# The opening of an encoder block: norm weights spread by TensorE, weight splits on ScalarE, and another order of loads and turns

## The chip, the cores and the metric

One core of a Trainium2 chip runs the kernel. The metric is the device time in microseconds (us) of one execution; lower is better. The engines run beside each other, each in the order of its own instruction list: TensorE (PE in the profile, its weight loads PEld), VectorE (DVE), ScalarE (ACT), GpSimd (POOL) and SyncE (SP), which issues the DMAs. They meet only at semaphores.

## The reference

One layer of an encoder on x of 1024 tokens by 1024 channels, all in float32:

```python
h = rmsnorm(x, norm_mix)                        # per token, times a gain per channel
proj = h @ w_in
qa, ka, va, ga, cq, ckv, kr, gb = split(proj, [512,128,128,512,384,256,32,512])
ya = window_attention(qa, ka, va, attn_sink) * silu(ga)
q  = rmsnorm(cq, q_a_norm) @ w_uq               # latent path of the second group of heads
kv = rmsnorm(ckv, kv_a_norm) @ w_ukv
yb = latent_attention(q, kv, rope(kr)) * silu(gb)
x  = x + concat(ya, yb) @ w_out
out = rmsnorm(x, final_norm)
```

The change touches only the first line and that part of the second which makes va, cq, ckv and kr.

## The kernel before

Every float32 product is made of three matmuls (`three`, L1097 to L1101): each operand is split into a rounded hi part and a lo part, and hi·hi, hi·lo and lo·hi are added up in PSUM. ps is PSUM, eight banks of 512 columns.

The opening stage works on tiles of 128 tokens, t = 0 to 7, and blocks of 128 input channels, k = 0 to 7.

- SP loads tile t of x into x_in (two buffers, L282) and block k of 800 of w_in's columns (va, ckv, kr, cq) into wn_raw (three buffers, three DMAs per block, L288 to L290). The gain norm_mix is read with each of the 128 partitions getting the whole vector, into g_mix (L293).
- ACT squares a tile with a running sum (L597), DVE makes the variance (L825), ACT the root (L600), DVE the reciprocal (L828) and then the normalised tile x_n, in one instruction over 1024 channels with g_mix (L831, semaphore s_xn).
- PE turns the tile with eight 128x128 transposes into banks 0 and 1 (`turn_x`, L1111; it waits for s_xn and for those banks to be read). ACT copies each half out as hT_hi (`h_hi`, L584), DVE subtracts for hT_lo (`h_lo`, L815, semaphore s_hT).
- POOL splits the weight blocks: wn_hi (L406), then wn_lo (L408, semaphore s_wnr).
- PE multiplies: `natural(t, c, ks)` adds block k of tile t into bank `nat_banks(t)[c]`, with 416 columns for c = 0 (va, ckv, kr) and 384 for c = 1 (cq). Tile t uses banks 2 and 3, 4 and 5, or 6 and 7, by t % 3. Three tiles are worked together, k by k, and between them the later tiles are turned; after k = 5 of the first three tiles all eight tiles have been turned, and k = 6 and 7 of tiles 0, 1 and 2 follow. Then tiles 3 to 7 follow one at a time.
- Tile 3 uses the banks of tile 0. It waits until tile 0's latent parts have been normalised out of them: ACT (L616 to L629), DVE (L851 to L866, semaphore s_lat).

```python
for t in range(3, NT):
    pe.wait_ge(s_hT, 2 * (t + 1))
    pe.wait_ge(s_lat, t - 2)
    natural(t, 0, range(KT))
```

On ACT, the list of the opening ends with `h_hi(NT - 1)` (L603), and the list that reads tile 0's banks begins after it (L613). On DVE it is the same with `h_lo(NT - 1)` (L836) and L848.

After this stage come the up-projections of the latents, windowed attention with the gated projections, latent attention and the output projection.

Of the kernel before, what the change touches and what calls it, by code (L numbers as in the profile page):

```python
# [32 lines left out]
P = 128  # L33
# [26 lines left out]
NA = P + KVL + ROPE  # L60
NW = NA + QL

# [9 lines left out]
def encoder(nc, x, norm_mix, w_in, attn_sink, q_a_norm, w_uq, kv_a_norm, w_ukv, w_out, final_norm,  # L72
# [7 lines left out]
    with ExitStack() as ctx:  # L80
# [21 lines left out]
        g_lat = at("g_lat", 144.5, [P, QL + KVL])  # L102
        lat = at("lat", 147, [P, 2, QL + KVL])
# [62 lines left out]
        ssq, var, rms, rstd = (stat[:, 8 * i:8 * i + 8] for i in range(4))  # L166
        lss, lvar, lrms, lrstd = (stat[:, 32 + 2 * i:34 + 2 * i] for i in range(4))
# [20 lines left out]
        s_wnh, s_wnr = sem("wn_hi_ready"), sem("wn_ready")  # L188
        s_pA, s_pB = sem("natA_done"), sem("natB_done")
# [88 lines left out]
        def _(sp):  # L278
            def load_x(t):
                if t >= 2:  # L280
                    sp.wait_ge(s_xn, t - 1)
                sp.dma_start(x_in[:, t % 2, :], x[t * P:(t + 1) * P, :]).then_inc(s_x[t % 2], 16)  # L282

            def load_wn(k):
                if k >= 3:
                    sp.wait_ge(s_wnr, k - 2)
                rows = w_in[k * P:(k + 1) * P, :]
                sp.dma_start(wn_raw[:, k % 3, 0:P], rows[:, VA:VA + P]).then_inc(s_wn[k % 3], 16)  # L288
                sp.dma_start(wn_raw[:, k % 3, P:NA], rows[:, CKV:CKV + KVL + ROPE]).then_inc(s_wn[k % 3], 16)
                sp.dma_start(wn_raw[:, k % 3, NA:NW], rows[:, CQ:CQ + QL]).then_inc(s_wn[k % 3], 16)  # L290
# [15 lines left out]
            sp.wait_ge(s_wnr, KT)  # L306
# [96 lines left out]
        def _(pool):  # L403
# [176 lines left out]
        def _(act):  # L580
# [10 lines left out]
            for t in range(NT):  # L591
                if t == 3:
                    h_hi(t - 1)
# [3 lines left out]
                nc.scalar.activation(x_n[:, t % 2, :], x_in[:, t % 2, :], ACT.Square,  # L597
                                     accum_out=ssq[:, t:t + 1]).then_inc(s_ssq, 1)
                act.wait_ge(s_var, t + 1)
                nc.scalar.activation(rms[:, t:t + 1], var[:, t:t + 1], ACT.Sqrt).then_inc(s_rms, 1)  # L600
                if t >= 1 and t != 3:
                    h_hi(t - 1)
            h_hi(NT - 1)  # L603
# [9 lines left out]
            for t in range(NT):  # L613
                a, b = nat_banks(t)
                act.wait_ge(s_pA, t + 1)
                nc.scalar.activation(vA[:, t, :, 0:HD], ps[:, a, 0:P].rearrange("p (g c) -> p g c", c=HD),  # L616
                                     ACT.Copy)
                if t >= 2:
                    act.wait_ge(s_lT, t - 1)
                nc.scalar.activation(lat[:, t % 2, QL:QL + KVL], ps[:, a, P:P + KVL], ACT.Square,  # L620
                                     accum_out=lss[:, 1:2])
                nc.scalar.activation(kr_n[:, t, :], ps[:, a, P + KVL:NA], ACT.Copy).then_inc(s_va, 1)
                act.wait_ge(s_pB, t + 1)
                nc.scalar.activation(lat[:, t % 2, 0:QL], ps[:, b, 0:QL], ACT.Square,
                                     accum_out=lss[:, 0:1]).then_inc(s_lss, 1)
# [177 lines left out]
        def _(dve):  # L803
# [17 lines left out]
            for t in range(NT):  # L821
                if t == 3:
                    h_lo(t - 1)
                dve.wait_ge(s_ssq, t + 1)
                nc.vector.tensor_scalar(var[:, t:t + 1], ssq[:, t:t + 1], 1.0 / D, EPS, ALU.mult,  # L825
                                        ALU.add).then_inc(s_var, 1)
                dve.wait_ge(s_rms, t + 1)
                link(nc.vector.reciprocal(rstd[:, t:t + 1], rms[:, t:t + 1]))  # L828
                if t == 0:
                    dve.wait_ge(s_gmix, 16)  # L830
                nc.vector.scalar_tensor_tensor(out=x_n[:, t % 2, :], in0=x_in[:, t % 2, :],  # L831
                                               scalar=rstd[:, t:t + 1], in1=g_mix[:, :], op0=ALU.mult,
                                               op1=ALU.mult).then_inc(s_xn, 1)
                if t >= 1 and t != 3:
                    h_lo(t - 1)
# [12 lines left out]
            for t in range(NT):  # L848
# [12 lines left out]
                nc.vector.scalar_tensor_tensor(out=lat[:, t % 2, 0:QL], in0=ps[:, b, 0:QL],  # L861
                                               scalar=lrstd[:, 0:1], in1=g_lat[:, 0:QL], op0=ALU.mult,
                                               op1=ALU.mult)
                nc.vector.scalar_tensor_tensor(out=lat[:, t % 2, QL:QL + KVL], in0=ps[:, a, P:P + KVL],
# [231 lines left out]
        def _(pe):  # L1096
# [7 lines left out]
            def turn_x(t):  # L1104
                pe.wait_ge(s_xn, t + 1)
                for a in range(2):
                    if t >= 1:
                        pe.wait_ge(s_hT, 2 * t - 1 + a)
                    for k in range(4):
                        c = 4 * a + k  # L1110
                        last = nc.tensor.transpose(ps[:, a, k * P:(k + 1) * P], x_n[:, t % 2, c * P:(c + 1) * P],  # L1111
                                                   ident[:, :])
                    last.then_inc(s_xT, 1)


            def natural(t, c, ks):
# [3 lines left out]
                for k in ks:  # L1120
                    last = three(ps[:, nat_banks(t)[c], 0:w1 - w0], hT_hi[:, k, toks], hT_lo[:, k, toks],
# [14 lines left out]

            pe.wait_ge(s_id, 2)

            turn_x(0)
            turn_x(1)  # L1140
# [12 lines left out]
            for t in range(3):  # L1153
                for c in range(2):
                    natural(t, c, range(KT - 2, KT))
# [256 lines left out]
```

## Time and profile before

| | |
|---|---|
| time before, median of 3 runs | 655.77 us (654.43 to 657.53) |
| profiled execution, first to last instruction | 655.6 us; no other time is given for it |
| PE busy | 633.3 us, 97% of the span |
| DVE busy | 403.8 us, 62% |
| ACT busy | 330.8 us, 50% |
| POOL busy | 302.5 us, 46% |
| idle before the turns of x on PE (L1111) | 7.9 us and 3.7 us |

The busy time of PE says how long matmuls were in flight, not how fast they went: its clock has two levels, and a matmul counts as busy at either. A line of the timeline gives the start in us, the length, the engine, the source line, the operation and its tiles; square brackets hold the idle time just before it and what ended that.

### The profile page before, as it was taken

The page shows a single profiled execution, that of the slowest core. Times are in us where ns is not written, and L with a number is a line of the kernel's source. Part 1 is how long each engine was busy: PE and PEld are TensorE (multiplying, and loading weights), DVE is VectorE, ACT ScalarE, POOL GpSimd, SP SyncE. Part 2 cuts the span into 40 slices and gives each one's busy share as a digit, 9 for nine tenths or more (in the row PEclk, how much of TensorE's full clock was granted, in tenths as well). Part 3 has the DMA queues.
Part 4 walks back from the last instruction along what each step waited for, and adds up shares of the span by engine and source line. Part 5 has one row for each costly group of instructions (what it writes and reads, how often), then busy time and mean ns, then how long its engine had stood idle before and what let it go on. Part 6 is the DMA issues. An engine that isn't in the chain of part 4 may idle for free.

```text
span 655.6 us, 8923 instructions
## 1 busy us (share of the span) xinstructions
PE 633.3 (97%) x3252; PEld 538.6 (82%) x3252; DVE 403.8 (62%) x773; ACT 330.8 (50%) x717; POOL 302.5 (46%) x283
## 2 busy tenths in 40 slices
PE   3999999999999999999999999999999999999996
PEld 2999998888888888788877788888888887888884
DVE  4753317333221158888885988888888888855422
ACT  4542222223222147777774877777777778404312
POOL 4962004402323244363535676886787777820000
PEclk9899999999999999999999999999999999999999
DMA  7730006363121210100123101011013201403521
GB/s 239 236 116 0 1 13 244 140 255 107 34 64 33 64 33 1 32 2 1 48 71 100 32 10 41 4 38 41 1 41 98 104 1 33 160 1 122 178 86 64
DMA packets 31612, 47.38 MB, mean 72 GB/s; under 512 B 2544, under 2 KB 19440, under 8 KB 31440
## 3 DMA queue, kind: packets, MB, share of 16 engines
q1 hardware_dynamic: 31568, 46.81, 22.7%
q8 instruction: 26, 0.43, 0.3%
q14 instruction: 18, 0.15, 0.1%
HBM read 35.13 MB, written 11.67 MB: 71 GB/s over the span
## 4 chain that ended last, share of the span: by engine, by line
PE 88%; DVE 6%; ACT 2%; DMA 1%; issue 1%; SPq 0%; DVEq 0%; ACTq 0%
PE ps L1099 21%; PE ps L1101 21%; PE ps L1100 21%; PE ps L1308 8%; PE ps L1324 4%; PE ps L1325 4%; PE ps L1251 2%; DVE p_w L934 2%; PE ps L1241 2%; PE ps L1252 1%; DVE pT_wl L962 1%; DVE o_w L972 1%; PE ps L1111 1%; DMA g_mix<-norm_mix 1%; DVE Y L921 1%
## 5 line engine op out<-in xcount | busy, mean ns | idle before, releaser
L523 POOL TENSOR_SCALAR p_b<-p_b,stat 128x1024 f32<-128x1024 f32 x64 | 72.0, 1126 | 52.8 <-DVE stat L1023 52.3
L738 ACT ACTIVATE pT_hi<-ps 128x512 fp32r<-128x512 f32 x128 | 69.9, 596 | 38.5 <-PE ps L1308 38.4
L1018 DVE TENSOR_REDUCE stat<-ps 128x1 f32<-128x1024 f32 x64 | 77.6, 1213 | 10.1 <-PE ps L1101 10.1
L1099 PE MATMUL ps<-hT_hi,w_hi 128*128 128x512 f32 x208 | 83.6, 402 | 0.0
L1028 DVE TENSOR_TENSOR pT_lo<-ps,pT_hi 128x512 fp32r<-128x512 f32 x128 | 81.8, 680 | 1.4 <-ACT pT_hi L738 1.4
L1101 PE MATMUL ps<-hT_hi,w_lo 128*128 128x512 f32 x208 | 81.3, 391 | 0.0
L1100 PE MATMUL ps<-hT_lo,w_hi 128*128 128x512 f32 x208 | 81.1, 390 | 0.0
L729 ACT ACTIVATE p_b<-ps,stat 128x1024 f32<-128x1024 f32 x64 | 71.5, 1117 | 12.0 <-DVE stat L1018 11.7
L1308 PEld LDWEIGHTS ps<-ident,p_b 128*128 128x128 f32 x512 | 59.3, 141 | 12.1 <-issue 2.6
L1308 PE MATMUL ps<-ident,p_b 128*128 128x128 f32 x512 | 67.3, 273 | 1.0 <-DVE pT_lo L1028 0.9
L466 POOL TENSOR_SCALAR p_w<-p_w,stat 128x384 f32<-128x384 f32 (+1 forms) x48 | 28.1, 602 | 60.9 <-DVE stat L949 60.9
L406 POOL TENSOR_SCALAR w_hi<-w_raw 128x1024 fp32r<-128x1024 f32 x13 | 14.1, 1083 | 91.1 <-PE ps L1101 91.1
L1324 PE MATMUL ps<-pT_hi,vB 128*128 128x512 f32 x128 | 55.3, 432 | 0.0
L1101 PE MATMUL ps<-k_hi,q_lo 96*128 96x512 f32 x128 | 50.5, 394 | 0.0
L1100 PE MATMUL ps<-k_lo,q_hi 96*128 96x512 f32 x128 | 50.5, 394 | 0.0
L1099 PE MATMUL ps<-k_hi,q_hi 96*128 96x512 f32 x128 | 50.3, 393 | 0.0
L1325 PE MATMUL ps<-pT_lo,vB 128*128 128x512 f32 x128 | 50.3, 393 | 0.0
L1101 PE MATMUL ps<-wo_hi,y_lo 128*128 128x512 f32 x128 | 49.8, 389 | 0.0
L1100 PE MATMUL ps<-wo_lo,y_hi 128*128 128x512 f32 x128 | 49.8, 389 | 0.0
L1099 PE MATMUL ps<-wo_hi,y_hi 128*128 128x512 f32 x128 | 49.8, 389 | 0.0
L1099 PE MATMUL ps<-wn_hi,hT_hi 128*128 128x384 f32 (+1 forms) x128 | 46.3, 362 | 0.0
L1101 PEld LDWEIGHTS ps<-hT_hi,w_lo 128*128 128x128 f32 x208 | 39.0, 188 | 8.5
(155 smaller groups left out, 1430.5 us busy)
## 6 DMA issues: line engine op xcount, KB each, us to landing
w_raw<-w_in SPq DMA_DIRECT2D x13, 512.0 KB, 3.9
x_in<-x SPq DMA_DIRECT2D x8, 512.0 KB, 4.5
wo_raw<-w_out SPq DMA_DIRECT2D x8, 512.0 KB, 4.0
x_r<-x SPq DMA_DIRECT2D x8, 512.0 KB, 3.9
out<-o_n SPq DMA_DIRECT2D x16, 256.0 KB, 2.3
q_nope_scratch<-stage SPq DMA_DIRECT2D x8, 256.0 KB, 2.9
k_nope_scratch<-stage SPq DMA_DIRECT2D x8, 256.0 KB, 2.1
v_scratch<-stage SPq DMA_DIRECT2D x8, 256.0 KB, 2.0
```

Of the source, the lines that this page charges most:

```text
L466: nc.gpsimd.tensor_scalar(p_w[:, u % 2, r, 0:w], p_w[:, u % 2, r, 0:w], w_col(5, u)[:, r:r + 1], 0.5, ALU.mult, ALU.mult).then_inc(s_wp, 1)
L523: nc.gpsimd.tensor_scalar(p_b[:, (U + 1) % 4, :], p_b[:, (U + 1) % 4, :], r_b[:, U % 4:U % 4 + 1], 0.5, ALU.mult, ALU.mult).then_inc(s_bp, 1)
L729: nc.scalar.activation(p_b[:, (U + 1) % 4, :], ps[:, b:b + 2, :].rearrange("p b c -> p (b c)"), ACT.Exp, bias=nm_b[:, U % 4:U % 4 + 1], ac ...
L738: nc.scalar.activation(pT_hi[:, G % 2, 4 * a:4 * a + 4, U % 4 * P:(U % 4 + 1) * P], ps[:, 4 + a, :].rearrange("p (k c) -> p k c", c=P), AC ...
L1018: nc.vector.tensor_reduce(nm_b[:, U % 4:U % 4 + 1], ps[:, b:b + 2, :].rearrange("p b c -> p (b c)"), AX.X, ALU.max, negate=True).then_inc( ...
L1028: nc.vector.tensor_tensor(pT_lo[at_], ps[:, 4 + a, :].rearrange("p (k c) -> p k c", c=P), f(pT_hi[at_]), ALU.subtract).then_inc(s_bTl, 1)
L1099: nc.tensor.matmul(o, a_hi, b_hi, start=first, stop=False)
L1100: nc.tensor.matmul(o, a_hi, b_lo, start=False, stop=False)
L1101: return nc.tensor.matmul(o, a_lo, b_hi, start=False, stop=last)
L1308: last = nc.tensor.transpose(ps[:, 4 + a, k * P:(k + 1) * P], p_b[:, (U + 1) % 4, (4 * a + k) * P:(4 * a + k + 1) * P], ident[:, :])
L1324: nc.tensor.matmul(o, vB[:, hp, k, :], pT_hi[:, G % 2, k, :], start=(k == 0), stop=False)
L1325: last = nc.tensor.matmul(o, vB[:, hp, k, :], pT_lo[:, G % 2, k, :], start=False, stop=(k == NT - 1))
```

## The change

- norm_mix is loaded as 8 rows of 128 (g_row, 4 KB). PE turns it to a column layout in bank 3, DVE copies it out (g_col), and PE spreads it with eight transposes of a broadcast column over banks 6 and 7. Tile 0 is normalised with the gain read from PSUM; ACT copies the two banks to g_mix for the other tiles (`keep_g`).
- Tile 0's squares are made half on ACT and half on DVE. All tiles are normalised in two instructions of 512 channels, each with its own increment of s_xn, and `turn_x` waits for each half.
- wn_hi is made by ACT (`wn_hi_k`), wn_lo by POOL in two parts (512 and 288 columns).
- The columns are divided anew: c = 0 holds va and cq (512), c = 1 holds ckv and kr (288); a block is loaded by two DMAs, not three. The steps that read the banks follow.
- Loads, ACT's list and PE's list stand in a new order. PE also does 8 and 4 transposes (`spin`) whose results nothing reads. The last turns of x are now spread among k = 4 to 7, and `turn_x(7)` is the last thing before tile 3.

```diff
-NA = P + KVL + ROPE
-NW = NA + QL
+NA = P + QL
+NW = NA + KVL + ROPE
...
             load_x(0)
-            sp.dma_start(g_mix[:, :], norm_mix.partition_broadcast(P)).then_inc(s_gmix, 16)
+            sp.dma_start(g_row[:, :], norm_mix.rearrange("(k c) -> k c", c=P)).then_inc(s_grow, 16)
+            load_wn(0)
             load_x(1)
-            load_wn(0)
             load_wn(1)
+            load_wn(2)
             load_x(2)
-            load_wn(2)
-            for t in range(3, NT):
-                load_wn(t)
-                load_x(t)
+            load_wn(3)
+            load_x(3)
+            load_wn(4)
+            load_wn(5)
+            load_x(4)
+            load_wn(6)
+            load_x(5)
+            load_wn(7)
+            load_x(6)
+            load_x(7)
...
             for k in range(KT):
-                pool.wait_ge(s_wn[k % 3], 48 * (k // 3 + 1))
-                split(wn_raw[:, k % 3, :], wn_hi[:, k, :], wn_lo[:, k, :], s_wnh, k + 1, s_wnr)
+                pool.wait_ge(s_wnh, k + 1)
+                for w0, w1 in ((0, NA), (NA, NW)):
+                    nc.gpsimd.tensor_tensor(wn_lo[:, k, w0:w1], wn_raw[:, k % 3, w0:w1], f(wn_hi[:, k, w0:w1]),
+                                            ALU.subtract).then_inc(s_wnr, 1)
...
+            def wn_hi_k(k):
+                act.wait_ge(s_wn[k % 3], 32 * (k // 3 + 1))
+                nc.scalar.activation(wn_hi[:, k, :], wn_raw[:, k % 3, :], ACT.Copy).then_inc(s_wnh, 1)
+
+            def keep_g(a):
+                act.wait_ge(s_xn, a + 1)
+                nc.scalar.activation(g_mix[:, a * HALF:(a + 1) * HALF], ps[:, 6 + a, :],
+                                     ACT.Copy).then_inc(s_gmix, 1)
+
+            square_x(0)
+            wn_hi_k(0)
+            keep_g(0)
+            h_hi(0)
+            keep_g(1)
+            square_x(1)
+            wn_hi_k(1)
+            h_hi(1)
+            wn_hi_k(2)
+            square_x(2)
...
+            square_x(7)
+            h_hi(6)
+            h_hi(7)
...
+            dve.wait_ge(s_gT, 1)
+            nc.vector.tensor_copy(g_col[:, :], ps[:, 3, 0:KT]).then_inc(s_gcol, 1)
+            for t in range(4):
+                norm_x(t)
+                if t < 3:
+                    h_lo(t)
+            for t in range(4, NT):
+                norm_x(t)
+                h_lo(t - 1)
...
             pe.wait_ge(s_id, 2)
+            spin(8)
+            pe.wait_ge(s_grow, 16)
+            nc.tensor.transpose(ps[:, 3, 0:KT], g_row[:, :], ident[0:KT, 0:KT]).then_inc(s_gT, 1)
+            pe.wait_ge(s_gcol, 1)
+            for a in range(2):
+                for k in range(4):
+                    last = nc.tensor.transpose(ps[:, 6 + a, k * P:(k + 1) * P],
+                                               g_col[:, 4 * a + k:4 * a + k + 1].to_broadcast([P, P]), ident[:, :])
+                last.then_inc(s_gb, 1)
+            spin(4)
 
             turn_x(0)
+            both(0, (0,))
             turn_x(1)
-            for k in range(KT - 2):
-                for t in range(3):
-                    if k == 0:
-                        pe.wait_ge(s_hT, 2 * (t + 1))
-                    pe.wait_ge(s_wnr, k + 1)
-                    for c in range(2):
-                        natural(t, c, range(k, k + 1))
-                    if k == 0 and t == 0:
-                        turn_x(2)
-                if k >= 1:
-                    turn_x(2 + k)
-            pe.wait_ge(s_wnr, KT)
-            for t in range(3):
-                for c in range(2):
-                    natural(t, c, range(KT - 2, KT))
+            both(0, (1,))
+            both(1, (0, 1))
+            both(0, (2,))
+            both(1, (2,))
+            turn_x(2)
+            both(0, (3,))
+            both(1, (3,))
+            both(2, range(4))
+            turn_x(3)
+            for k in range(4, KT):
+                for t in range(3):
+                    both(t, (k,))
+                turn_x(k)
             for t in range(3, NT):
                 pe.wait_ge(s_hT, 2 * (t + 1))
                 pe.wait_ge(s_lat, t - 2)
```

`both(t, ks)` is `natural(t, 0, ...)` and `natural(t, 1, ...)` for each k of ks.

## Rows read from the trace of the kernel before

**Rows 1.** The page: busy time of each engine over the span.
```profile
PE 633.3 (97%) x3252; PEld 538.6 (82%) x3252; DVE 403.8 (62%) x773; ACT 330.8 (50%) x717; POOL 302.5 (46%) x283
```

**Rows 2.** Waits of PE, whole span: us in total, times, longest.
```profile
PE ps L1111 <- DVE x_n L831: 7.9, 1, 7.9
PE ps L1111 <- DVE hT_lo L815: 3.7, 2, 2.0
PE ps L1251 <- DVE pT_wl L962: 1.4, 4, 0.5
```

**Rows 3.** The chain of waits, 0 to 20 us: start, length, what.
```profile
1.18 5.19 DMA g_mix<-norm_mix
...
6.48 1.29 DVE x_n L831
...
7.79 4.35 DMA x_in<-x
...
13.97 2.50 DVE x_n L831
16.47 0.61 DVE hT_lo L815
...
17.22 1.24 PE ps L1111 x8
```

**Rows 4.** Timeline, 4 to 26 us.
```profile
4.03 1.06 ACT L597 ACTIVATE x_n<-x_in 128x1024 f32<-128x1024 f32 x1 [1.80 <-DMA x_in<-x]
5.00 0.19 ACT L597 ACTIVATION_READ_ACCUMULATOR x_n<-x_in 128x1 f32 x1
5.21 0.15 DVE L825 TENSOR_SCALAR stat<-stat 128x1 f32<-128x1 f32 x1 [5.21 <-ACT x_n L597]
5.40 0.20 ACT L600 ACTIVATE stat<-stat 128x1 f32<-128x1 f32 x1 [0.22 <-DVE stat L825]
5.64 0.17 DVE L828 RECIPROCAL stat<-stat 128x1 f32<-128x1 f32 x1 [0.27 <-ACT stat L600]
...
7.91 1.94 PE L1111 MATMUL ps<-ident,x_n 128*128 128x128 f32 x8 [7.91 <-DVE x_n L831]
...
8.83 0.86 POOL L406 TENSOR_SCALAR wn_hi<-wn_raw 128x800 fp32r<-128x800 f32 x1 [7.36 <-DMA wn_raw<-w_in]
...
9.56 1.28 DVE L831 SCALAR_TENSOR_TENSOR x_n<-x_in,stat,g_mix 128x1024 f32<-128x1024 f32 x1
...
14.91 0.34 PE L1101 MATMUL ps<-wn_hi,hT_lo 128*128 128x384 f32 x1
```

**Rows 5.** Groups by shape, 0 to 50 us: busy in all, mean ns of one, idle before.
```profile
L408 POOL TENSOR_TENSOR wn_lo<-wn_raw,wn_hi 128x800 fp32r<-128x800 f32 x8 | 17.0, 2128 | 0.7
...
L815 DVE TENSOR_TENSOR hT_lo<-ps,hT_hi 128x512 fp32r<-128x512 f32 x16 | 10.3, 686 | 6.7 <-ACT hT_hi L584 6.6
...
L584 ACT ACTIVATE hT_hi<-ps 128x512 fp32r<-128x512 f32 x16 | 8.8, 595 | 13.7 <-PE ps L1111 13.6
```

**Rows 6.** Busy time and granted clock (the number before the last two) by stretch.
```profile
18.20:21.50 3.30, 3.30 (x12) 3.20 (x11) 2.34 (x5) 2.12 (x5) 3.22 (x3) 0.50 0.88 285
22.00:26.00 4.00, 4.00 (x26) 3.93 (x25) 2.57 (x4) 1.25 (x4) 3.92 (x2) 1.00 0.52 158
```

**Rows 7.** Timeline, 37 to 50 us.
```profile
37.73 1.04 PE L1111 MATMUL ps<-ident,x_n 128*128 128x128 f32 x8
38.37 1.09 ACT L584 ACTIVATE hT_hi<-ps 128x512 fp32r<-128x512 f32 x2 [1.61 <-PE ps L1111]
38.53 0.43 PE L1099 MATMUL ps<-wn_hi,hT_hi 128*128 128x416 f32 x1
...
44.10 0.28 ACT L616 ACTIVATE vA<-ps 128x128 fp32r<-128x128 f32 x1 [0.48 <-PE ps L1101]
...
45.15 0.49 ACT L624 ACTIVATE lat<-ps 128x384 f32<-128x384 f32 x1 [0.32 <-PE ps L1101]
...
46.98 0.47 DVE L864 SCALAR_TENSOR_TENSOR lat<-ps,stat,g_lat 128x256 f32<-128x256 f32 x1
...
47.13 0.35 PE L1099 MATMUL ps<-wn_hi,hT_hi 128*128 128x416 f32 x1
...
49.32 0.35 PE L1099 MATMUL ps<-wn_hi,hT_hi 128*128 128x416 f32 x1
```

More of the change, by code:

```diff
@@ L102, in encoder @@
         g_lat = at("g_lat", 144.5, [P, QL + KVL])
+        g_row = at("g_row", 201, [KT, P])
+        g_col = at("g_col", 204, [P, KT])
         lat = at("lat", 147, [P, 2, QL + KVL])
@@ L590, in _, with square_x @@
             nc.scalar.activation(oss[:, 0:1], ident[:, 0:1], ACT.Sqrt)
-            for t in range(NT):
-                if t == 3:
-                    h_hi(t - 1)
+            def square_x(t):
                 act.wait_ge(s_x[t % 2], 16 * (t // 2 + 1))
@@ L596, in _ @@
                     act.wait_ge(s_xT, 2 * (t - 1))
-                nc.scalar.activation(x_n[:, t % 2, :], x_in[:, t % 2, :], ACT.Square,
-                                     accum_out=ssq[:, t:t + 1]).then_inc(s_ssq, 1)
+                if t == 0:
+                    nc.scalar.activation(x_n[:, 0, 0:HALF], x_in[:, 0, 0:HALF], ACT.Square, scale=D ** -0.5,
+                                         accum_out=ssq[:, 0:1]).then_inc(s_ssq, 1)
+                else:
+                    nc.scalar.activation(x_n[:, t % 2, :], x_in[:, t % 2, :], ACT.Square,
+                                         accum_out=ssq[:, t:t + 1]).then_inc(s_ssq, 1)
                 act.wait_ge(s_var, t + 1)
                 nc.scalar.activation(rms[:, t:t + 1], var[:, t:t + 1], ACT.Sqrt).then_inc(s_rms, 1)
-                if t >= 1 and t != 3:
-                    h_hi(t - 1)
-            h_hi(NT - 1)
+            def wn_hi_k(k):
[15 more added lines that the diff above has]
+            square_x(2)
+            wn_hi_k(3)
+            h_hi(2)
+            wn_hi_k(4)
+            square_x(3)
+            wn_hi_k(5)
+            square_x(4)
+            h_hi(3)
+            wn_hi_k(6)
+            square_x(5)
+            h_hi(4)
+            wn_hi_k(7)
+            square_x(6)
+            h_hi(5)
+            square_x(7)
+            h_hi(6)
+            h_hi(7)
             def lat_hi(t):
@@ L818, in h_lo, with norm_x @@
                                             ALU.subtract).then_inc(s_hT, 1)
[L821 to L826, printed above, removed]
+            def norm_x(t):
+                if t == 0:
+                    dve.wait_ge(s_x[0], 16)
+                    link(nc.vector.tensor_tensor_reduce(out=x_n[:, 0, HALF:], in0=x_in[:, 0, HALF:],
+                                                        in1=x_in[:, 0, HALF:], scale=1.0 / D, scalar=EPS,
+                                                        op0=ALU.mult, op1=ALU.add, accum_out=sq_b))
+                    dve.wait_ge(s_ssq, 1)
+                    nc.vector.tensor_tensor(var[:, 0:1], ssq[:, 0:1], sq_b, ALU.add).then_inc(s_var, 1)
+                else:
+                    dve.wait_ge(s_ssq, t + 1)
+                    nc.vector.tensor_scalar(var[:, t:t + 1], ssq[:, t:t + 1], 1.0 / D, EPS, ALU.mult,
+                                            ALU.add).then_inc(s_var, 1)
@@ L827, in _ @@
                 dve.wait_ge(s_rms, t + 1)
                 link(nc.vector.reciprocal(rstd[:, t:t + 1], rms[:, t:t + 1]))
[L829 to L835, printed above, removed]
+                for a in range(2):
+                    cols = slice(a * HALF, (a + 1) * HALF)
+                    if t == 0:
+                        dve.wait_ge(s_gb, a + 1)
+                        gain = ps[:, 6 + a, :]
+                    else:
+                        dve.wait_ge(s_gmix, a + 1)
+                        gain = g_mix[:, cols]
+                    nc.vector.scalar_tensor_tensor(out=x_n[:, t % 2, cols], in0=x_in[:, t % 2, cols],
+                                                   scalar=rstd[:, t:t + 1], in1=gain, op0=ALU.mult,
+                                                   op1=ALU.mult).then_inc(s_xn, 1)
```

45 lines of the change are left out of this document (29 added, 16 removed).

## The prediction

> **What bounds the kernel now.** I read the page first: PE is busy for 97% of the span, everything else for 62% or less [rows 1]. So only time in which PE stands still or runs slowly can be won. The waits of PE say where it stands still: 7.9 us before the first turn of x and 3.7 us before the next two; the next entry, far later, is 1.4 us in all [rows 2]. The change can win only in the first 17 us. The chain of waits names what is late there, in turn: the 512 KB of g_mix, DVE's first x_n, tile 2 of x, and DVE's x_n of tile 2, which took 2.50 us where the neighbouring one in the timeline took 1.28 [rows 3, 4]. From 17.22 on PE has work without a break.
>
> The third view is the clock. In the stretch 18.2 to 21.5 the granted clock is 0.50, the lower level, and in 22 to 26 it is 1.00 [rows 6]; before it fell PE had stood still from 15.25 to 17.22 [rows 3, 4]. At the lower level 12 matmuls started in 3.3 us, at the upper 26 in 4.0, or 21.5 in 3.3. The 9.5 missing ones at 0.154 us are 1.5 us, and over a whole low stretch of some 3.5 us about 1.7. The first eight transposes took 1.94 us, those at 37.73 1.04 [rows 4, 7]: the opening also runs slowly.
>
> A yardstick: `natural` of tile 3 begins at 49.32 [rows 7]. From 17.22 to there PE did six turns and 23 of the 24 (tile, k) pairs of the first three tiles, in 32.1 us, of which 1.7 us is the low clock: 30.4 us of work at full clock. What the change does to this 49.32 it does to the end, since PE is without notable waits after it.
>
> **The change part by part.**
>
> *Size of the matmuls.* Twelve of them (two pairs) take 49.32 - 47.13 = 2.19 us [rows 7], 1.09 us a pair. 512 + 288 columns are as many as 416 + 384. One of 400 columns on average takes 0.1825, of which 0.167 are its columns at 2.4 GHz, the upper level, and 0.016 are fixed; 288 columns would need 0.12 + 0.016. I take no change; if a matmul of 288 columns cost as much as one of 384, it would be 3 x 0.04 us (96 columns) x 64 pairs = 7.7 us. Against that speaks that a weight load and its 128-column transpose go through in 1.04/8 = 0.13 us [rows 7], no more than 288 columns need anyway, so a load does not hold them up. I give 0, upper end +1 us.
>
> *The first tile.* g_mix landed at 6.37; without it x_n(0) would have been possible at 5.8 [rows 3, 4]. In its place: x_in lands at 4.03, g_row behind it, at 4.1 to 4.2; a turn (0.4), DVE's copy (0.2), and four transposes at the slow rate (1.2) make the first half of the gain ready at 6.1, the second at 6.9. DVE first has to wait for the turned g_row, and only then sums its half of the squares (0.7, as a 512-wide operation of L815), so the variance comes at 5.7, the root at 6.1, the reciprocal at 6.3. The halves of x_n(0) end at 7.0 and 7.7. The spins end at 7.5, and the turn begins there: 0.4 us earlier than 7.91. The change does what its first item says, but the 512 KB were replaced by a chain nearly as long. Bounds: 7.1 (spin at full clock) to 9.0 (g_row as late as g_mix's 6.37 [rows 3]; I take 4.2, since it is 4 KB and not 512).
>
> *ACT's list, what is late next.* Behind tile 0's root (6.1) come now wn_hi(0) (0.85: 800 columns between 0.56 for 512 and 1.06 for 1024 [rows 4, 5]; to 6.95), keep_g(0) (from 7.0, to 7.6), h_hi(0) (its halves wait for the turn, 8.65 and 9.5 at the slow rate; to 10.1), keep_g(1) (to 10.6), and only then the square of tile 1, which has lain in x_in since about 6.6. Square to x_n ready to start took 4.03 to 5.83, 1.8 us [rows 4]: x_n(1) runs from 12.4 to 13.8. Before, it ran from 9.56 to 10.84 [rows 4]. Tile 1 is thus 3 us later than before; tile 2, which held PE up before, no longer does (x_n(2) at 18.2 to 19.5 against a turn at 20). wn_hi(1) follows at 12.2, wn_lo(1) on POOL ends in two parts at 14.3 and 15.1 (2.1 us in all [rows 5]). Turn 1 is done at 14.1 to 14.6, and the pair (0, k=1) can start at about 14.6. Bounds: 13.9 with everything before at full clock, 16.0 if DVE's halves and POOL stretch each other as the 2.50 us instruction shows [rows 3].
>
> *From there.* Six turns and 23 pairs are left, the same as at 17.22 before. I followed the lists on: wn_lo(2) at 17.6 and 18.4 against 17.9 and 18.6; hT(2) at 21.9 against 23.1; the turns of tiles 3 to 7 and the blocks k = 4 to 7 are ready 1.5 to 4 us ahead. Moving wn_hi to ACT takes 8 x 1.35 us from POOL, which then waits on ACT; ACT has room (8.8 us of copies in 50). The x loads now stand behind weight loads in SP's queue, which wait for s_wnr; x(4) goes out at about 20 for a square at 27. No cover is lost. So the work ends at 14.6 + 30.4 = 45.0 without any low clock, 46.7 with the same 1.7 us as before; I take 45.9. That is 3.4 us ahead of 49.32.
>
> *The stall before tile 3.* Before, the last turn was at 41.89 and twelve pairs' worth of matmuls, 6.6 us, stood behind it before tile 3. Now `turn_x(7)` is the last thing before it. ACT's and DVE's lists read tile 0's banks only behind h_hi(7) and h_lo(7), which wait for that very turn; and tile 3 waits for tile 0's latents. So a chain that had lain under matmuls lies open. With S the start of the turn: h_hi(7) ends at S + 1.73 (37.73 to 39.46); PE would go on at S + 0.80 (38.53) [rows 7]. From vA's start to the end of the last latent instruction took 44.10 to 47.45, 3.35 us, with 0.32 us of waiting for PE in it [rows 7], so 3.03. PE goes on at S + 1.73 + 3.03 + 0.1 = S + 4.85 and has stood still 4.05 us. The new division of columns orders the same instructions otherwise, to the same sum. The only cover is none; the bounds are 3.7 and 4.4.
>
> *The clock behind the stall.* A stop of 1.97 us was followed by a low stretch worth 1.7 us [rows 3, 4, 6]. This stop is twice as long, so I charge 1.7 again; lower bound 0.
>
> *Sum.* Tile 3 effectively begins at 45.9 + 4.05 + 1.7 = 51.65 against 49.32: +2.3 us. The span is 655.6 and the median of the runs 655.77, so nothing is lost between the two; 655.77 + 2.3 = 658.0.
>
> One point on the clock could move this. In the trace the lower rate held through 16 transposes and ended at about 14.5, a bit over a microsecond after the first matmuls of the pairs had begun; that the transposes helped to raise the clock is likely, since they made up most of what PE had done, but one trace does not prove it. The Trainium skill, "TensorE: Matmul & The Clock Gate", Part 4, says that transposes do not count as PE activity for the clock in the way matmuls do. By that rule the spins and the spreading of the gain raise nothing, and the opening is slow throughout; what that costs here is the third rival.
>
> **The rivals.**
> 1. *Forecast: stall and low clock outweigh the earlier start.* Around +2.3 us, 656.5 to 659.5. Chance 0.45.
> 2. *Full clock all through; not slower.* PE is nearly without a break from 4.9 to 9.3 us in the new list. If that brings the upper level before 9 us, and the stop before tile 3 does not cost it, the work starts at 13.9, ends at 44.3, and tile 3 begins at 48.4: -1.0 us, 654.8. It decides at a low-clock cost under 1 us in all. For it: after 14.5 the full rate came and lasted over a 2 us stop, until 18.2. Against: it then fell. Chance 0.2. A gain of over 0.5% needs the stall to be absent as well, by a cover that I overlook: 3.4 to 5 us ahead, 651.5; chance 0.05.
> 3. *Transposes leave the clock low; slower.* Turns 0 and 1 and the first pairs at half rate: start at 15.3, the full 1.7 us, end at 47.4; then 4.05 and 1.7: 53.15, +3.8 us, 659.6. The page named above is the reason to hold this apart. For it: the first 16 transposes were all slow, and the clock fell at 18.2 after turns and a stop. Chance 0.2.
> 4. *POOL and DVE in each other's way.* x_n halves and wn_lo stretched as in the 2.50 us case: start at 16.0, +1.4 us on the forecast, 659.5 or, with rival 3, 661. Chance 0.1.
>
> **How the numbers follow.** About 0.5% (3.3 us) is what a measurement of this kernel tells from no change; the three runs before lie 3.1 us apart. Slower by more than that, over 659.1: nearly all of rivals 3 and 4 (0.28) and a tenth of the forecast's case, 0.33. Faster by more, under 652.5: 0.05. The same: the rest, 0.62. The range 653.8 to 661.2 reaches from rival 2, with the spread of the runs below it, to rivals 3 and 4 together.
>
> **What would show it.** Right: PE's waits show one new entry of about 4 us before L1099 at 45 to 47 us, ended by DVE's latents (L930 or so), the granted clock is low after it, and the first wait before a turn ends at 7.5. ACT's square of tile 1 starts at 10 to 11 us, not on landing. Wrong: no such entry; or a second stop between 16 and 45 us, which would mean that ACT's list is the bound; or the first pairs already at the full rate, which would make rival 2 true; or 288-column matmuls spaced wider than 0.14 us.

## The result and the profile after

The changed kernel takes 662.67 us (661.97 to 662.71, 4 runs) against 656.54 us of the kernel before (654.43 to 657.53, 4 runs): a ratio of 1.0092, 95% interval [1.0077, 1.0107]. It is slower by 6.1 us. Forecast were 658.0 us and +2.3 us; the sign and the stall were right, the price of the low clock was not, and the time lies above the range. The profiled executions are 660.9 and 655.6 us long, 5.3 us apart.

The page of the changed kernel, busy time of each engine, beside [rows 1]:

```profile
PE 640.7 (97%) x3273; PEld 536.6 (81%) x3273; DVE 405.6 (61%) x784; ACT 337.0 (51%) x727; POOL 292.6 (44%) x283
```

Waits of PE in the changed kernel (us in total, times, longest), beside [rows 2]:

```profile
PE ps L1166 <- DVE lat L931: 3.9, 1, 3.9
PE ps L1178 <- DVE x_n L890: 2.6, 2, 1.7
```

The 7.9 and 3.7 us before the turns have become 2.6 (and 1.5 before the first spin, which costs nothing). A new entry stands on top: 3.9 us before the first matmul of tile 3 (L1166), ended by DVE's latents. It is the stall that the prediction placed there.

Timeline of the opening, beside [rows 3, 4]:

```profile
5.88 1.52 DVE L890 SCALAR_TENSOR_TENSOR x_n<-x_in,stat,ps 128x512 f32<-128x512 f32 x2
...
7.27 1.91 PE L1178 MATMUL ps<-ident,x_n 128*128 128x128 f32 x8
...
9.74 0.50 PE L1166 MATMUL ps<-wn_hi,hT_hi 128*128 128x512 f32 x1 [0.56 <-DVE hT_lo L862]
...
10.19 1.06 ACT L611 ACTIVATE x_n<-x_in 128x1024 f32<-128x1024 f32 x1
...
11.99 2.42 DVE L890 SCALAR_TENSOR_TENSOR x_n<-x_in,stat,g_mix 128x512 f32<-128x512 f32 x2
...
15.24 0.78 PE L1166 MATMUL ps<-wn_hi,hT_hi 128*128 128x512 f32 x1
...
15.81 0.63 PE L1167 MATMUL ps<-wn_lo,hT_hi 128*128 128x512 f32 x1
...
16.24 0.63 PE L1168 MATMUL ps<-wn_hi,hT_lo 128*128 128x512 f32 x1
...
20.14 0.39 PE L1168 MATMUL ps<-wn_hi,hT_lo 128*128 128x512 f32 x1
```

The reader is to see four things. The turn of tile 0 starts at 7.27, 0.6 us earlier than before. The first pair, at 9.74, already runs at the full rate (0.23 us between its 512-column matmuls). ACT squares tile 1 only at 10.19, and its two normalising instructions, beside POOL's wn_lo, take 2.42 us, where the same two of a later tile took 1.41 (at 35.01, with POOL idle); before, x_n(1) was ready at 10.84, now at 14.4. And the matmuls from 15.24 on are 0.43 us apart instead of 0.23: they run at half rate until 20.14. By the granted clock the low stretch is longer: it begins at 13.2 and ends at 20.0. (In the first microseconds that column is no guide: it reads 1.00 from 5 to 9 us, where the transposes were 0.21 us apart, against 0.11 at full rate in experiment 1. There the rate is read from the spacing.)

Timeline around the stall, beside [rows 7]:

```profile
46.98 1.03 PE L1178 MATMUL ps<-ident,x_n 128*128 128x128 f32 x8
...
48.59 0.28 ACT L663 ACTIVATE vA<-ps 128x128 fp32r<-128x128 f32 x1
...
51.27 0.47 DVE L931 SCALAR_TENSOR_TENSOR lat<-ps,stat,g_lat 128x256 f32<-128x256 f32 x1
...
51.89 0.77 PE L1166 MATMUL ps<-wn_hi,hT_hi 128*128 128x512 f32 x1 [3.88 <-DVE lat L931]
...
57.57 0.40 PE L1167 MATMUL ps<-wn_lo,hT_hi 128*128 128x512 f32 x1
```

Turn of tile 7 at 46.98, tile 0's first copy on ACT behind h_hi(7) at 48.59, the last latent instruction at 51.27, tile 3 at 51.89 and not 49.32. From there 13 matmuls of 512 columns take 5.68 us, to 57.57. Busy time by stretch, the granted clock being the number before the last two, beside [rows 6]:

```profile
15.20:19.80 4.60, 4.60 (x15) 3.94 (x14) 2.14 (x5) 3.36 (x6) 2.57 (x3) 0.50 0.60 203
...
48.00:51.70 3.70, 0.02 (x1) 0.00 (x0) 2.83 (x9) 3.09 (x15) 3.42 (x10) 0.87 0.01 2
51.70:57.20 5.50, 5.31 (x13) 4.18 (x14) 1.54 (x7) 0.37 (x2) 5.50 (x8) 0.50 0.00 0
```

At full rate (0.23 us apart) the 13 would take 3.0 us, so this low stretch costs 2.7 us. The one in the opening, 15.24 to 20.14, holds 8 matmuls of 512 and 6 of 288 columns, 8 x 0.23 + 6 x 0.13 = 2.6 us of work in 4.9: 2.3 us lost.

The account by the yardstick: tile 3 begins 2.57 us later than before, its first matmuls lose 2.7 us more, together 5.3 us, which is the whole difference of the two profiled executions.

### The profile page after: what moved, and what is told of

It is laid out like the page before. It is cut to its first block, busy times and chain, and to the rows that moved or that the text cites. A ratio compares the mean times of both kernels' runs of the same rounds, so it can differ in the third digit from the quotient of the medians.

```text
span 660.9 us, 8993 instructions
## 1 busy us (share of the span) xinstructions
PE 640.7 (97%) x3273; PEld 536.6 (81%) x3273; DVE 405.6 (61%) x784; ACT 337.0 (51%) x727; POOL 292.6 (44%) x283
## 4 chain that ended last, share of the span: by engine, by line
PE 89%; DVE 6%; ACT 2%; issue 2%; DMA 0%; SPq 0%; DVEq 0%; ACTq 0%
PE ps L1166 21%; PE ps L1168 21%; PE ps L1167 21%; PE ps L1400 8%; PE ps L1417 4%; PE ps L1416 4%; PE ps L1343 2%; DVE p_w L1001 2%; PE ps L1333 2%; PE ps L1344 1%; PE ps L1178 1%; DVE pT_wl L1029 1%; DVE o_w L1039 1%; PE ps L1322 1%; PE ps L1321 1%
## 5 line engine op out<-in xcount | busy, mean ns | idle before, releaser
L1085 DVE TENSOR_REDUCE stat<-ps 128x1 f32<-128x1024 f32 x64 | 77.6, 1213 | 10.2 <-PE ps L1168 10.1
L1166 PE MATMUL ps<-hT_hi,w_hi 128*128 128x512 f32 x208 | 83.6, 402 | 0.0
L1166 PE MATMUL ps<-wn_hi,hT_hi 128*128 128x288 f32 (+1 forms) x128 | 47.4, 370 | 4.4 <-DVE lat L931 3.9
L1166 PE MATMUL ps<-k_hi,q_hi 96*128 96x512 f32 x128 | 50.3, 393 | 0.0
L1166 PE MATMUL ps<-wo_hi,y_hi 128*128 128x512 f32 x128 | 49.8, 389 | 0.0
```

The source lines that it names most:

```text
L1085: nc.vector.tensor_reduce(nm_b[:, U % 4:U % 4 + 1], ps[:, b:b + 2, :].rearrange("p b c -> p (b c)"), AX.X, ALU.max, negate=True).then_inc( ...
L1166: nc.tensor.matmul(o, a_hi, b_hi, start=first, stop=False)
```

## The experiments

All times are medians; the ratios are to the kernel before on the same chip, which took 657.3 to 657.4 us in these three groups of runs, with their 95% intervals. Experiments 1, 2 and 4 to 6 make one edit to the changed kernel and 3 makes one to the kernel before; the others build on 2 and 8. The changed kernel was not run again in these groups: in its own group the kernel before took 656.54. So a difference "under the changed kernel" compares two groups and is sure to about 1 us; the spans of the traces and the starts inside them are given beside it where it matters.

**1. Two pairs of cover.** The turns of tiles 4 to 7 one place earlier.

```diff
             for k in range(4, KT):
                 for t in range(3):
                     both(t, (k,))
-                turn_x(k)
+                    if t == 0:
+                        turn_x(k)
```

> The changed kernel, but the turns of tiles 4 to 7 stand behind the first of the three pairs of their k instead of the third, so two pairs (2.2 us) of matmuls cover the chain before tile 3. Theory (the stall and the low clock behind it are the loss): the stop before tile 3 shrinks from 3.9 to about 1.7 us, 2.2 us less; if the clock then stays up, 2.6 us more are won: 2.2 to 4.8 us under the changed kernel. Rival (the opening is what costs, the turns are needed as late as they are): a new stop before the turns of tiles 4 to 7 takes the place of the one removed and the time stays within 1 us of the changed kernel.

657.4 us, ratio 1.0006 [0.9997, 1.0015]: 5.3 us under the changed kernel, and level with the kernel before. Its waits of PE:

```profile
PE ps L1178 <- DVE x_n L890: 2.4, 2, 1.3
PE ps L1166 <- DVE lat L931: 1.7, 1, 1.7
```

The stop before tile 3 is 1.7 us, tile 3 begins at 49.03, and the clock stays at 1.00 from 18.2 us on. 2.2 us fewer of stop and 2.7 us of low clock make 4.9 us; the spans are 5.5 apart (655.4 against 660.9). The other 0.6 are of the opening, where this execution's low stretch is shorter (14.7 to 18.1) though its first 20 us are the same code. The rival falls: the waits before turns did not grow.

**2. Four pairs of cover.**

```diff
-                turn_x(k)
+                    if t == 0 and k < 7:
+                        turn_x(k)
+                    if t == 1 and k == 6:
+                        turn_x(7)
```

> The changed kernel, but the turn of tile 7 already behind the second pair of k = 6, the turns of 4 to 6 behind the first pair of their k: four pairs (4.4 us) cover the chain before tile 3. Theory: no stop before tile 3 and no low clock after it, 3.9 + 2.6 = 6.5 us under the changed kernel, which is then 0 to 1.5 us under the kernel before. Rival: the turns come too early, PE waits before them instead, and no more than half is won.

657.28 us, 1.0004 [0.9994, 1.0013], 5.4 us under the changed kernel. The stop before tile 3 is 0.7 us. The expected 6.5 us were not reached; beyond the first two pairs of cover nothing measurable is added. The rival does not explain it: the waits before the turns are 2.3 us, against 2.6 in the changed kernel. The 0.7 us that are left of the stop are not the turn's any more, as ACT's first copy out of tile 0's bank shows:

```profile
46.59 0.28 ACT L663 ACTIVATE vA<-ps 128x128 fp32r<-128x128 f32 x1 [1.19 <-PE ps L1168]
```

It waits for the last matmul of tile 0, behind which the new order has two pairs before tile 3, where the kernel before had four. And the opening goes two ways: five of the ten runs, with a mean granted clock (over the whole run) of 0.993 or 0.994, took 657.5 to 658.1 us, the other five (0.996 to 0.998) 656.4 to 657.0. The profiled one is of the first kind, low from 12.6 to 19.5 us. So in this form, without the turn's stall, the rest of the change is worth about nothing, not the 3.4 us by which I had put it ahead.

**3. The stall alone, in the kernel before.**

```diff
-                if k >= 1:
+                if 1 <= k < 5:
                     turn_x(2 + k)
             pe.wait_ge(s_wnr, KT)
             for t in range(3):
                 for c in range(2):
                     natural(t, c, range(KT - 2, KT))
+            turn_x(7)
```

> The kernel before with one edit: the turn of tile 7 is moved behind all 24 pairs, directly ahead of tile 3. Theory: 4 us of stop and 1.7 to 2.6 us of low clock, 5.7 to 6.6 us slower than the kernel before, as much as the whole change costs. Rival (the stall is harmless, because PE is ahead of something else later): under 2 us slower.

662.09 us, 1.0084 [1.0062, 1.0106], 4.7 us over the kernel before by the medians, 5.5 by the ratio; a little less than I expected. One moved turn costs nearly as much as the whole change. The new entry among the waits of PE, then the stretches of the stop and behind it:

```profile
PE ps L1099 <- DVE lat L864: 3.6, 1, 3.6
```

```profile
48.80:52.40 3.60, 0.02 (x1) 0.00 (x0) 2.96 (x9) 3.09 (x15) 3.35 (x9) 1.00 0.01 2
53.00:57.00 4.00, 4.00 (x15) 3.84 (x14) 1.08 (x3) 0.04 (x1) 4.00 (x7) 0.59 0.01 4
```

A stop of 3.6 us, then a granted clock of 0.59 on average over 4 us (0.41 x 4 = 1.6 us lost), at a place where the kernel before has neither: the stall brings the low clock with it. The opening of this run is the code of the kernel before, and in this trace it has no low stretch, where that of the kernel before has one from 18.2 to 21.6 us [rows 6].

**4. Filling the stall.** Matmuls that nothing reads, on bank 0 as soon as it is free.

```diff
                 turn_x(k)
+            pe.wait_ge(s_hT, 2 * NT - 1)
+            for _ in range(12):
+                nc.tensor.matmul(ps[:, 0, :], hT_hi[:, 0, 0:P], wn_hi[:, 0, 0:HALF], start=True, stop=True)
```

> The changed kernel with 12 matmuls of 512 columns, whose results nothing reads, in the stop before tile 3 (from when bank 0 is free, about 1 us into it, to its end). Theory (the low clock is a cost of its own, caused by PE standing still): the stretch at a granted clock of 0.50 after the stop goes, the start of tile 3 stays where it is or comes up to 0.3 us later, and the kernel is 2.3 to 2.6 us faster than the changed one. Rival (the low clock there comes by itself, or from something else that happens then): no gain, or a loss by the extra matmuls.

659.73 us, 1.0037 [1.0023, 1.005], 2.9 us under the changed kernel:

```profile
48.74 2.99 PE L1250 MATMUL ps<-wn_hi,hT_hi 128*128 128x512 f32 x12 [0.98 <-DVE hT_lo L862]
51.63 0.47 PE L1166 MATMUL ps<-wn_hi,hT_hi 128*128 128x512 f32 x1
51.94 0.40 PE L1167 MATMUL ps<-wn_lo,hT_hi 128*128 128x512 f32 x1
```

PE does work for nothing from 48.74 on, tile 3 starts 0.3 us earlier than in the changed kernel, and its matmuls are 0.23 us apart from the second on. The low clock behind the stop is a cost of its own, of 2.7 us by the trace and 2.9 by the times, and it is PE's standing still that causes it. (The opening has its low stretch here too, 12.6 to 19.4 us, and in four of the five runs the mean granted clock is 0.992; the fifth, with 0.999, took 658.5 us.)

**5. Filling the gap of the opening.**

```diff
             both(0, (0,))
+            for _ in range(7):
+                nc.tensor.matmul(ps[:, 4, :], hT_hi[:, 0, 0:P], wn_hi[:, 0, 0:HALF], start=True, stop=True)
             turn_x(1)
```

> The changed kernel with 7 matmuls of 512 columns, whose results nothing reads, between the first pair and the turn of tile 1, where PE stands still for 1.7 us. Theory (the low stretch from about 14 to 20 us is caused by PE standing still for the halves of tile 1): the granted clock stays at 1.00, the pairs from 15 us on go at full rate, and up to 2.3 us are won against the changed kernel. Rival (the clock falls there whatever PE does in that gap, or the second gap alone brings it down): within 0.5 us of the changed kernel.

659.16 us, 1.0021 [1.0012, 1.0031], 3.5 us under the changed kernel. Two pieces of PE's timeline:

```profile
10.71 1.78 PE L1235 MATMUL ps<-wn_hi,hT_hi 128*128 128x512 f32 x7
...
14.28 0.48 PE L1166 MATMUL ps<-wn_hi,hT_hi 128*128 128x512 f32 x1
14.60 0.39 PE L1167 MATMUL ps<-wn_lo,hT_hi 128*128 128x512 f32 x1
```

```profile
48.96 0.77 PE L1166 MATMUL ps<-wn_hi,hT_hi 128*128 128x512 f32 x1 [3.88 <-DVE lat L931]
...
52.08 0.42 PE L1167 MATMUL ps<-wn_lo,hT_hi 128*128 128x512 f32 x1
```

The pairs from 14.28 on run at full rate, against half rate until 20.14 in the changed kernel. The stall is as long as ever (48.96 is its end), but the low stretch behind it is shorter: 7 matmuls in 3.12 us, 1.5 us lost instead of 2.7. The profiled execution is 4.1 us shorter than the changed kernel's (656.8 against 660.9): tile 3 begins 2.9 us earlier, and 1.2 less is lost behind the stall. Of the 2.9, about 2 are the clock from the second pair on; that pair also starts 1.0 us earlier, but not because of the edit alone, since in experiment 1, without it, it started at 14.37. What a stop of 3.9 us costs in clock is not one number: 1.5 and 2.7 us were seen. Both forms of the rival are out: with the gap of 1.7 us filled the clock stays up in this trace and in that of experiment 7, though the second gap (1.0 us) is still there, while all four traces with the gap as it was (the changed kernel, experiments 1, 2 and 4) have a low stretch.

**6. Without the spins.**

```diff
             pe.wait_ge(s_id, 2)
-            spin(8)
...
-            spin(4)
```

> The changed kernel without the 8 and the 4 spins. Theory (transposes do raise the clock; in the changed kernel the first pair at 9.7 us went at the full rate with nothing but transposes before it): the first pair goes at the half rate and the turn of tile 0 starts 0.2 us earlier; the time changes by less than 1 us, since PE waits for tile 1 anyway. Rival (spins do nothing at all): the first pair still at the full rate, no change of time.

659.77 us (658.65 to 662.45), 1.0043 [1.0026, 1.006], 2.9 us under the changed kernel, where I expected less than 1 us either way. PE's timeline:

```profile
6.63 1.97 PE L1178 MATMUL ps<-ident,x_n 128*128 128x128 f32 x8
9.15 0.80 PE L1166 MATMUL ps<-wn_hi,hT_hi 128*128 128x512 f32 x1 [0.56 <-DVE hT_lo L862]
9.75 0.63 PE L1167 MATMUL ps<-wn_lo,hT_hi 128*128 128x512 f32 x1
...
16.52 0.30 PE L1168 MATMUL ps<-wn_hi,hT_lo 128*128 128x288 f32 x1
...
50.00 0.47 PE L1166 MATMUL ps<-wn_hi,hT_hi 128*128 128x512 f32 x1 [3.88 <-DVE lat L931]
50.30 0.39 PE L1167 MATMUL ps<-wn_lo,hT_hi 128*128 128x512 f32 x1
...
54.18 0.39 PE L1168 MATMUL ps<-wn_hi,hT_lo 128*128 128x512 f32 x1
```

The first pair is at half rate (0.43 us between the 512-column matmuls, 0.23 with spins), as the theory had it. But the clock comes up at 16.5 and stays, while with spins it came up before 9.7, fell before 14 and was low until 20.14. My reading is that the spins raise the clock too early for a PE that then stands still for 1.7 us (0.7 here, where the slower matmuls and transposes fill the time). Only part of the gain is of the opening, though. By the traces (658.0 against 660.9 us) tile 3 begins 1.9 us earlier, and the rest lies behind the stall: ten steps from 50.30 to 54.18 take 3.9 us instead of 2.3, 1.6 us lost instead of 2.7. And it is partly luck: six of the eight runs took 658.65 to 660.37 us with a mean granted clock of 0.995 or 0.996, but two took 661.9 and 662.45 us with 0.988 and 0.987, the time and the clock of the changed kernel (0.988 in all four of its runs).

**7. Cover and filling together.** The edits of 2 and 5.

> The turns of e2_four_pairs together with the filling matmuls of e5_fill_opening. Theory (two causes that add up): 6.0 us (cover, as measured in e2) and up to 2.3 us (clock in the opening) under the changed kernel, so 1 to 2 us under the kernel before. Rival (the opening's clock is made up for by waits behind it): the same time as e2_four_pairs, within 0.5 us.

655.64 us, 0.9965 [0.9952, 0.9978], 7.0 us under the changed kernel and 1.6 us under e2. Each edit is worth something beside the other, and this is the first version under the kernel before. But they do not simply add up: alone they brought 5.4 and 3.5 us, and what the filling wins behind the stall cannot be won again where the stall is covered. Tile 3 begins at 47.27.

**8. Tile 1's squares on DVE.** With the turns of 2, without filling matmuls.

```diff
             keep_g(0)
             h_hi(0)
-            keep_g(1)
             square_x(1)
+            keep_g(1)
             wn_hi_k(1)
...
                 norm_x(t)
+                if t == 0:
+                    dve.wait_ge(s_x[1], 16)
+                    nc.vector.tensor_tensor_reduce(out=x_n[:, 1, :], in0=x_in[:, 1, :], in1=x_in[:, 1, :],
+                                                   scale=1.0 / D, scalar=EPS, op0=ALU.mult, op1=ALU.add,
+                                                   accum_out=var[:, 1:2]).then_inc(s_var, 1)
```

(`square_x(1)` keeps only the root, and `norm_x(1)` no longer makes the variance.)

> The turns of e2_four_pairs, and tile 1's squares made on DVE instead of ACT, with ACT's root for tile 1 straight behind the hi halves of tile 0. Theory (ACT's list is what holds tile 1 back: its square started at 10.2 though the tile had landed before 8): x_n of tile 1 starts at 10.6 to 11 instead of 12.0, the second pair 1.0 to 1.6 us earlier, PE's gap is shorter and the clock may stay up: 1 to 3.5 us under e2_four_pairs. Rival (wn_lo of block 1 on POOL holds the second pair, not tile 1): x_n(1) earlier, but the second pair no more than 0.5 us earlier and no gain.

654.4 us, 0.9947 [0.9933, 0.9962]: 8.3 us under the changed kernel, 2.9 under e2, 2.9 under the kernel before. Timeline:

```profile
7.79 1.40 DVE L903 CUSTOM_DVE_ANT_0 x_n<-x_in 128x1024 f32<-128x1024 f32 x1 [0.34 <-DMA x_in<-x]
...
10.63 2.43 DVE L893 SCALAR_TENSOR_TENSOR x_n<-x_in,stat,g_mix 128x512 f32<-128x512 f32 x2
...
13.53 0.48 PE L1174 MATMUL ps<-wn_hi,hT_hi 128*128 128x512 f32 x1
...
13.85 0.39 PE L1175 MATMUL ps<-wn_lo,hT_hi 128*128 128x512 f32 x1
```

The squares start when tile 1 lands (7.79), x_n(1) at 10.63 and not 11.99, the second pair at 13.53 (14.37 to 15.29 in the four traces with the old opening) and at full rate. Tile 3 begins at 46.12. The rival falls, and ACT's list was what held the opening back.

**9. Experiment 8 without the spins** (the diff of 6).

> e8_squares_on_dve without its 12 spins. Theory (the spins do raise the clock, and in the changed kernel they only raised it too early to last): the first pair and the turn of tile 1 go at half rate and the clock comes up near 16 us, as in e6_no_spins; 1 to 2 us slower than e8. Rival (spins only cost): as fast as e8 or faster.

654.7 us, 0.9956 [0.9942, 0.9971]; the interval overlaps that of e8, which is from another group (the kernel before took 657.28 and 657.29 us in the two). The first pair is at half rate at 10.23 and the second, at 14.14, at full. Where the gaps are short the spins neither cost nor bring anything that can be measured; the forecast of 1 to 2 us was a miss.

**10. The gain by DMA again, in experiment 8.**

```diff
-            sp.dma_start(g_row[:, :], norm_mix.rearrange("(k c) -> k c", c=P)).then_inc(s_grow, 16)
+            sp.dma_start(g_mix[:, :], norm_mix.partition_broadcast(P)).then_inc(s_gmix, 16)
...
             spin(8)
...
-            spin(4)
+            spin(13)
```

(That makes 21 spins; there are 21 transposes before the turn of tile 0 in experiment 8 too. The turn of g_row, the spreading, the copies g_col and keep_g are gone; tile 0 reads g_mix too.)

> e8_squares_on_dve, but the gain comes by a DMA of 512 KB as in the kernel before; PE does 13 spins in place of spins and spreading, ACT copies no gain. Theory (the spreading by TensorE is worth little, since ACT's list and not the gain set the pace): x_n(0) starts at 6.4 to 6.5 instead of 5.9, block 0 of the weights lands 1.5 us later and the first pair starts 1 us later; 0 to 1.5 us slower than e8. Rival (the 512 KB are what the opening waited for): 2 us or more slower than e8.

657.1 us, 0.9994 [0.9985, 1.0004], 2.7 us slower than e8. That is the rival's figure, not mine. Timeline:

```profile
6.47 1.41 DVE L890 SCALAR_TENSOR_TENSOR x_n<-x_in,stat,g_mix 128x512 f32<-128x512 f32 x2 [1.10 <-DMA g_mix<-norm_mix]
...
7.59 0.87 ACT L621 ACTIVATE wn_hi<-wn_raw 128x800 fp32r<-128x800 f32 x1 [2.42 <-DMA wn_raw<-w_in]
...
8.55 3.00 POOL L431 TENSOR_TENSOR wn_lo<-wn_raw,wn_hi 128x512 fp32r<-128x512 f32 x2 [7.08 <-ACT wn_hi L621]
...
11.56 0.79 PE L1169 MATMUL ps<-wn_hi,hT_hi 128*128 128x512 f32 x1 [2.32 <-POOL wn_lo L431]
```

x_n(0) starts at 6.47, half a us later than with the spread gain. But block 0 of the weights lands at 7.59, its wn_lo ends at 11.55, and the first pair waits for that until 11.56, against 9.86. PE has then stood still for 2.3 us, and it runs at half rate until 17.5, where experiment 8 was at full rate from 9.86 on. Tile 3 begins 3.0 us later (49.12): 1.7 are the late first pair, and how the rest is shared between the low clock and the chain behind it this run does not tell. The worth of the first item of the change lies less in the gain than in the 512 KB that no longer stand in front of the weights.

**11. wn_hi on POOL, in experiment 8** (`wn_hi_k` on ACT is empty).

```diff
-                pool.wait_ge(s_wnh, k + 1)
+                pool.wait_ge(s_wn[k % 3], 32 * (k // 3 + 1))
+                nc.gpsimd.tensor_scalar(wn_hi[:, k, :], wn_raw[:, k % 3, :], 1.0, 1.0, ALU.mult,
+                                        ALU.mult).then_inc(s_wnh, 1)
+                pool.wait_ge(s_wnh, k + 1)
```

> e8_squares_on_dve, but wn_hi is made by POOL as in the kernel before. Theory (ACT's list is what is tight, POOL has room): POOL needs 0.9 to 1.8 us more for each block; block 1 is ready at about 13.5 to 14.5 as before and the time stays within 1 us of e8. Rival (POOL becomes the bound of the weights in the opening): PE waits for wn_lo of blocks 1 to 3 and it is 2 us or more slower than e8.

654.51 us, 0.9952 [0.9937, 0.9967]: as fast as e8, although the first pair waits 1.4 us for POOL's wn_lo and starts at 10.16 at half rate. Where wn_hi is made does not matter once tile 1 no longer waits for ACT.

**12. POOL behind DVE, in experiment 8.**

```diff
                 pool.wait_ge(s_wnh, k + 1)
+                if k == 1:
+                    pool.wait_ge(s_xn, 4)
```

> e8_squares_on_dve, but POOL's wn_lo of block 1 waits for both halves of x_n(1). Theory (the two halves took 2.43 us instead of 1.41 because POOL's two-operand instruction ran beside them): x_n(1) takes 1.4 to 1.5 us, the turn of tile 1 ends 1 us earlier, wn_lo(1) ends about 0.4 us later, and the time stays within 0.5 us of e8 since the second pair needs both. Rival (the halves are slow by themselves in that place): 2.4 us again, and 1 to 2 us slower than e8.

654.24 us, 0.9949 [0.9932, 0.9965], the time of e8. Timeline:

```profile
10.36 1.42 DVE L895 SCALAR_TENSOR_TENSOR x_n<-x_in,stat,g_mix 128x512 f32<-128x512 f32 x2
```

x_n(1) takes 1.42 us, not 2.43: the longer time is the price of running beside POOL's subtraction. The second pair comes at 13.26 instead of 13.53, so nearly nothing of the 1 us arrives: it now waits for wn_lo(1).

## Why the prediction was wrong in size, point by point

The step that failed is the price of the low clock, in two terms of the sum: 1.7 us behind the stall where 2.7 were lost, and 0.9 us in "From there" where 2.3 were lost. A smaller third is the start of that work, 0.6 us later than forecast. The stall itself was forecast rightly.

- *The stall before tile 3* was right in place, cause and size: 4.05 us forecast, 3.88 measured. Experiments 1 to 4 show it by cover, by transplanting it and by filling it. (The cover of 6.6 us that the prediction calls twelve pairs' worth is six pairs, twelve blocks of three matmuls; the time is right.)
- *The clock behind the stall* is a term that was mis-sized: 1.7 us charged, copied from the one low stretch of [rows 6], 2.7 measured. Experiment 4 isolates it at 2.9 us. The case copied was not a bad one: behind the same kind of stop (3.6 to 3.9 us) experiments 3, 5 and 6 lost 1.6, 1.5 and 1.6 us. Why the changed kernel lost 2.7 is open. The 1.7 itself rests on a count that compares unlike things, since some six of the 26 starts from 22 to 26 us are short transposes; that it nearly stands all the same is luck: the ten steps from 18.14 to 21.61 took 3.47 us, at full rate about 1.9, so 1.6 us were lost.
- *"From there": the low clock in the opening* was mis-sized more: 0.9 us charged, half of what the kernel before loses, 2.3 measured; experiment 5 shows that PE's gap of 1.7 us before the turn of tile 1 causes it. I had counted on the new list keeping PE busier. It does until 11.1 us; then tile 1, which the same step put 3 us later, leaves the gap. Its size changes from execution to execution: with the same code in the first 20 us the clock was low from 13.2 to 20.0, 14.7 to 18.1, 12.6 to 19.5 and 12.6 to 19.4 us (the changed kernel, experiments 1, 2, 4).
- *ACT's list* was right in kind: the square of tile 1 starts at 10.2, forecast 10.6. The start of the second pair came at 15.2 instead of 14.6, within the bound of 16.0, because rival 4 was true: x_n(1) starts 0.4 us earlier than forecast (11.99) but takes 2.42 us beside POOL, 1.0 more. The clock has a hand in that start too: in experiment 1, with x_n(1) as slow (2.43), the pair started at 14.37, since the turn of tile 0 took 1.35 us instead of 1.91 and the second half of tile 1's 0.66 instead of 1.11. In experiment 12, without the stretching, the pair gained only 0.3 us, because it then waits for wn_lo(1). Experiment 8 shows that list to be what the opening waits for.
- These three make the account: work ready for tile 3 at 47.8 instead of 45.9 (0.6 by the start, 1.4 by the clock behind it), stall and hand-over 4.1 instead of 4.05, low clock 2.7 instead of 1.7. Together 5.3 us against 2.3.
- *The baseline* was a step that failed in a small way. I took the median of three runs, 655.77, to belong to the span of 655.6. In every run of the changed kernel time and span are 1.8 us apart (662.67 and 660.9), and the kernel before came to 657.3 to 657.4 in the later groups of runs, 1.8 us over its 655.6. With that the same sum would have read 659.7. It does not bear on the difference of 5.3 us, only on its distance to the 6.1 of the medians.
- *The size of the matmuls* was right: the 288-column matmuls are 0.13 us apart, the pair 1.09 to 1.10 us.
- *The gain*: the turn of tile 0 started at 7.27, forecast 7.5. That the new path saves little was right for tile 0 and missed its second effect, 1.7 us on the weights of block 0 (they land at 7.59 in experiment 10 and at 5.88 in experiment 8).
- *A sign that misled.* The prediction names the first pairs at the full rate as what would make rival 2 true. The first pair was at the full rate (9.74), and rival 2 did not follow: the clock fell at 13.2.
- *Rival 3 and the rule on transposes.* Together with rival 4 it gave 661, the nearest to the measured time, but not by its mechanism. In the changed kernel only transposes had run before 9.74, and the first pair ran at full rate; without the 12 spins it ran at half rate (experiment 6, and again 9). In experiments 1 and 5 the turn of tile 0 took 1.35 and 1.30 us instead of 1.91: the clock came up in the middle of it, before any matmul. So transposes do bring the clock up here, though not in every run: of the nine traces with these 21 transposes ahead of the turn, eight have the first pair at full rate and experiment 11 has it at half, at 10.16 after a wait of 1.4 us; so has experiment 10, with 21 spins and a wait of 2.3 us. The rule of the Trainium skill ("TensorE: Matmul & The Clock Gate", Part 4), that they do not count as activity in that way, is not borne out by these runs.

Not tried: the changed kernel with the stall removed on ACT's and DVE's side, by reading tile 0's banks ahead of h_hi(7) and h_lo(7). What decides how long a low stretch lasts is open; the traces show losses from 1.5 to 2.7 us and not a law.

## What to carry to other kernels

When a step is moved to the end of one engine's list, look at what the other engines' lists have behind the instruction that waits for it: here ACT and DVE could not read tile 0's banks until the last turn was done, and the six pairs (6.6 us) of matmuls that had covered the hand-over were gone. In a kernel that lives on PE, count a stop twice, once as time and once as the low clock behind it, take for the second a range and not one earlier case, and ask it of every gap that a change opens. An item that saves a DMA may pay on what stood behind it in the queue. And before one trace explains a difference of 1 us, look at the mean granted clock of all the runs.

## What the runs showed of the hardware that was not expected

- A gap of 1.7 us (11.1 to 12.8) and at most a half turn of 0.4 us behind it stood ahead of a fall of the clock at 13.2 that lasted to 20.0 (2.3 us lost from the second pair on), in a PE that had been busy from 4.65 to 9.2 and from 9.74 on. In experiment 2 the clock fell at 12.6, still within the gap.
- The same stop of 3.9 us cost 2.7 us of clock in one kernel and 1.5 and 1.6 us in two others (experiments 5 and 6).
- Transposes alone brought the clock up: in experiment 1 the transposes of the first turn were 0.21 us apart and then, from the fourth on, 0.11, with no matmul before them.
- Raising the clock early did not help a kernel in which PE then stood still (spins: 662.67 us, without 659.77, with two of eight runs as slow as with them).
- Two 512-column instructions of DVE with two inputs took 1.42 us alone and 2.43 us beside a two-input instruction of POOL.
